# Two mixer stages folded into the feed-forward units block by block, with a unit's first side step ahead of the unit's own waits

## What is computed

```
h    = rms_norm(x) * (1 + scale1) + shift1
proj = h @ w_in                       # split over three causal mixers
out_a = rg_lru(conv(xa)) * gelu(ya)   # A, recurrent
out_b = forgetting_attention(rms_norm(fq), rms_norm(fk), fv, ff)   # B, "fox": 6 heads of 64
out_c = gated_linear_attention(gq, gk, gv, glow, gg)               # C, "gla": 4 heads, chunks of 64
x = x + gate1 * (concat(out_a, out_b, out_c) @ w_out)
h = rms_norm(x) * (1 + scale2) + shift2
x = x + gate2 * ((silu(h @ w_gate) * (h @ w_up)) @ w_down)
```

## Time and profile before

| | before |
|---|---|
| median of 3 runs | 3176.07 us (3166.4 to 3176.65) |
| profiled execution, its own time | 3180.37 us |
| span of the profile | 3178.6 us |
| share of the span: PE, DVE, ACT, POOL | 90%, 44%, 38%, 32% |
| mean granted TensorE clock | 0.925 of 2.4 GHz |

### The profile page before, as it was taken

How to read it: one execution, slowest core, us unless ns; L and a number is a source line. 1 busy time by engine, 2 the same in 40 slices (tenths; PEclk the granted TensorE clock), 3 DMA queues, 4 the chain that set the end, 5 groups by cost and what they waited for, 6 DMA issues and landing times.

```text
span 3178.6 us, 32439 instructions
## 1 busy us (share of the span) xinstructions
PE 2845.1 (90%) x12416; PEld 2258.7 (71%) x12416; DVE 1404.6 (44%) x1753; ACT 1206.8 (38%) x1601; POOL 1028.7 (32%) x466
## 2 busy tenths in 40 slices
PE   8899999935565579999999999998999999999999
PEld 4687878712344558888877887886878787778887
DVE  3878774543553543433334433334444443341112
ACT  3333242241523235354434445342444545232222
POOL 3545454400000023333333333333322223344443
PEclk9999999965556589999999999999999999999999
DMA  7555444357103424343444343443444343433233
GB/s 258 172 169 186 151 147 130 132 242 231 78 14 132 115 89 139 105 140 115 126 128 142 117 141 110 142 132 111 152 117 143 122 123 107 126 103 95 97 99 93
DMA packets 143866, 418.74 MB, mean 132 GB/s; under 512 B 16306, under 2 KB 18114, under 8 KB 137406
## 3 DMA queue, kind: packets, MB, share of 16 engines
q1 hardware_dynamic: 140848, 411.28, 40.7%
q10 hardware_dynamic: 2768, 5.24, 0.4%
q0 software_dynamic: 96, 0.15, 0.0%
HBM read 355.69 MB, written 60.92 MB: 131 GB/s over the span
## 4 chain that ended last, share of the span: by engine, by line
PE 59%; DVE 3%; issue 2%; DMA 2%; ACT 1%; SPq 1%; POOL 0%; DVEq 0%; ACTq 0%; POOLq 0%
PE ff_acc_ps L77 16%; PE ff_acc_ps L78 16%; PE ff_acc_ps L79 16%; PE fa_o_ps L1667 2%; PE fa_st_ps L1653 2%; PE fa_s_ps L1629 2%; PE fa_o_ps L1669 2%; PE fa_st_ps L1654 2%; PE fa_o_ps L1668 2%; PE fa_s_ps L1630 1%; DMA out_yT<-ff_gated 1%; DVE ff_silu L1480 1%; DVE ff_h_lo L1470 0%; DVE ff_rstd L1474 0%; DMA ff_silu<-mix_dram 0%
## 5 line engine op out<-in xcount | busy, mean ns | idle before, releaser
L1356 POOL TENSOR_TENSOR ff_w_lo<-ff_w_raw,ff_w_hi 128x1024 fp32r<-128x1024 f32 (+1 forms) x304 | 716.0, 2355 | 1450.1 <-PE ff_acc_ps L79 1422.5
L77 PE MATMUL ff_acc_ps<-ff_h_hi,ff_w_hi 128*128 128x512 f32 x1664 | 659.0, 396 | 42.8 <-DVE ff_h_lo L1470 21.4
L78 PE MATMUL ff_acc_ps<-ff_h_lo,ff_w_hi 128*128 128x512 f32 x1664 | 655.7, 394 | 0.0
L79 PE MATMUL ff_acc_ps<-ff_h_hi,ff_w_lo 128*128 128x512 f32 x1664 | 655.0, 394 | 0.0
L1365 ACT ACTIVATE ff_w_hi<-ff_w_raw 128x1024 fp32r<-128x1024 f32 (+1 forms) x304 | 315.6, 1038 | 853.2 <-PE ff_acc_ps L79 802.8
L77 PEld LDWEIGHTS ff_acc_ps<-ff_h_hi,ff_w_hi 128*128 128x128 f32 x1664 | 316.6, 190 | 117.4 <-issue 24.3
L79 PEld LDWEIGHTS ff_acc_ps<-ff_h_hi,ff_w_lo 128*128 128x128 f32 x1664 | 316.0, 190 | 68.2
L78 PEld LDWEIGHTS ff_acc_ps<-ff_h_lo,ff_w_hi 128*128 128x128 f32 x1664 | 316.7, 190 | 66.4
L1510 DVE TENSOR_TENSOR fa_p_lo<-fa_probs,fa_p_hi 128x512 fp32r<-128x512 f32 x240 | 146.5, 612 | 427.5 <-ACT fa_p_hi L1402 427.1
L209 POOL TENSOR_TENSOR w_lo<-w_raw,w_hi 128x1024 fp32r<-128x1024 f32 x96 | 240.0, 2502 | 272.5 <-PE g_ps L79 219.5
L77 PE MATMUL g_ps<-h_hi,w_hi 128*128 128x512 f32 x768 | 307.7, 401 | 16.9 <-POOL w_lo L209 12.8
(11 more groups left out here) (229 smaller groups left out, 3938.0 us busy)
## 6 DMA issues: line engine op xcount, KB each, us to landing
ff_w_raw<-in_w_gate_up SPq DMA_DIRECT2D x176, 512.0 KB, 3.8
w_raw<-in_w_in SPq DMA_DIRECT2D x96, 512.0 KB, 4.0
ff_w_raw<-in_w_down SPq DMA_DIRECT2D x64, 512.0 KB, 4.8
mod_w<-in_w_mod SPq DMA_DIRECT2D x24, 1024.0 KB, 5.5
fa_v<-v_split_dram SPq DMA_DIRECT2D x60, 384.0 KB
proj_dram<-stage SPq DMA_DIRECT2D x72, 256.0 KB, 3.2
ff_w_raw<-in_w_out SPq DMA_DIRECT2D x32, 512.0 KB, 4.9
fa_ks_a<-ka_dram SPq DMA_DIRECT2D x60, 256.0 KB
```

Source lines behind the costliest of these rows:

```text
L77: nc.tensor.matmul(out, hi, act_hi, start=first, stop=False)
L78: nc.tensor.matmul(out, hi, act_lo, start=False, stop=False)
L79: return nc.tensor.matmul(out, lo, act_hi, start=False, stop=last)
L1356: nc.gpsimd.tensor_tensor(w_lo[:, j % LO, wide], w_raw[:, j % RAW, wide], w_hi[:, j % HI, wide].bitcast(F32), ALU.subtract).then_inc(lo_re ...
```

## The change

`fox_operands` and `gated_linear_attention` are gone as functions of their own. The new `mix_and_feed_forward` does both for one block of 512 tokens at a time, as side steps: 7 steps "X" (operands) and 2 x 8 steps "G" (a head pair of mixer C). Block 0's 23 steps stand, one after another, ahead of the units and of block 0's attention. The steps of blocks 1, 2 and 3 stand one to a unit among the units of the block before (X in units 4 to 10, G in 14 to 29 for block 1, and 83 to 89 and 93 to 108 for block 2), and the block's attention turns follow in what is left: 34, 31 and 31 units. Carries (`f_carry`, `carry`) go from block to block. The buffers of X, of G, of attention and of the output projection's input share one region of SBUF, so each has to wait for the stores or the readers of the one before it (`operands_done`, `g_out`, `filled`, `heads_done`). The eight tiles of the output projection's input are now loaded together. The first turn of a unit now stands ahead of the unit's waits, and the others at even parts.

```diff
-def fox_operands(nc, vec, consts, fox_rows, proj, q_split, ka, kb, v_split):
...
-def gated_linear_attention(nc, vec, consts, w_alpha, proj, mix):
...
-def attend_and_feed_forward(nc, vec, mod, xT, w_out, w_gate_up, w_down, consts, mix, q_split, ka, kb, v_split, yT):
+def mix_and_feed_forward(nc, vec, mod, xT, w_alpha, w_out, w_gate_up, w_down, consts, fox_rows, proj, mix, q_split, ka, kb, v_split, yT):
...
+    X_STEPS, G_STEPS, X_LEAD, G_LEAD, A_LEAD, END = 7, 8, 3, 3, 2, 6
...
+    for b in range(NBLK):
+        turns = turns_of(b)
+        lo = -PRE if b == 0 else 1 if b == 1 else at["o", b - 1, KD - 1, 0] + 1
+        x_load.append(lo)
+        lo += X_LEAD
+        for s in range(X_STEPS):
+            side[lo + s] = [[("X", (b, s))]]
+        lo += X_STEPS + 1
+        g_load.append(lo)
+        lo += G_LEAD - 1
+        for j in range(GLA_T):
+            for s in range(G_STEPS):
+                side[lo + G_STEPS * j + s] = [[("G", (b, j, s))]]
+        lo += GLA_T * G_STEPS + 1
+        a_load.append(lo)
+        lo += A_LEAD - 1
+        hi = 0 if b == 0 else at["o", b, 0, 0] - END
         for x, turn in enumerate(turns):
             side.setdefault(lo + x * (hi - lo) // len(turns), []).append(turn)
...
+                def load_mix(b):
+                    heads_done(sp, b)
+                    for k in range(KD):
+                        sp.dma_start(mix_raw[:, k], mix[k, :, cols(b)]).then_inc(mix_in[k], 16)
...
+                    if kind == "G":
+                        b = n
+                        operands_done(sp, b)
+                        sp.dma_start(glow[:], proj[T_MISC, 0:GLA_RANK, cols(b)]).then_inc(glow_in, 16)
...
+                def ones(b):
+                    pool.wait_ge(g_out, 16 * GLA_T * (b + 1))
+                    nc.gpsimd.memset(q_b[HEAD_DIM:].bitcast(F32), 1.0).then_inc(filled, 1)
...
                     for x, turn in enumerate(turns):
-                        turn_at.setdefault((x + 1) * K // (len(turns) + 1), []).append(turn)
+                        turn_at.setdefault(x * K // len(turns), []).append(turn)
+                    for turn in turn_at.pop(0, []):
+                        attend(turn)
                     pe.wait_ge(lo_ready, j + 1)
```

More of the change, by code:

```diff
@@ new lines, in mix_and_feed_forward @@
+        with region:
+            qk, v_raw, sqr = there("fp_qk", [P, TILES, BLK]), there("fp_v_raw", [P, FOX_T, BLK]), there("fp_squares", [P, 3, BLK])
+            rows = [there("fp_rows%d" % i, [FF_ROW + FOX_HEADS, BLK]) for i in range(4)]
+            bias_hi, bias_lo = (there("fp_bias_" + n, [FF_ROW + FOX_HEADS, BLK], F32R)[FF_ROW:] for n in ("hi", "lo"))
+            qk_hi, qk_lo = there("fp_hi", [P, 2, BLK], F32R), there("fp_lo", [P, 2, BLK], F32R)
+            v_nat = there("fp_v_nat", [P, 2, 2, TPB, 3 * HEAD_DIM], F32R)
@@ new lines, in mix_and_feed_forward @@
+        region = ExitStack()
+        with region:
+            gk, gq, gv, gg = (there("ga_" + n, [P, GLA_T, BLK]) for n in ("gk", "gq", "gv", "gg"))
+            glow, restart = there("ga_glow", [GLA_RANK, BLK]), there("ga_restart", [P, BLK])
+            z, e_neg, one_e, b_cum, grow = (there("ga_" + n, [P, BLK]) for n in ("z", "e_neg", "one_e", "b_cum", "grow"))
+            v_n, k_n = there("ga_v_n", [P, TPB, P]), there("ga_k_n", [P, TPB, P])
+            att, state = there("ga_att", [P, 2, TPB, P]), there("ga_state", [P, NCH + 1, P])
@@ new lines, in mix_and_feed_forward @@
+        region = ExitStack()
+        with region:
+            mix_raw = there("ff_mix_raw", [P, KD, BLK])
+            raw_consts = there("fa_raw_consts", [P, 2, P])
+        mean, rstd12, newton = (r[0:HEADS2] for r in rows[:3])
+        logit, f_exp, log1p, f_err = (r[FF_ROW:FF_ROW + FOX_HEADS] for r in rows)
+        ones_row = ones_col[FF_ROW:FF_ROW + FOX_HEADS].to_broadcast([FOX_HEADS, BLK])
+        v_hi, v_ones, v_lo = (v_nat[:, :, :, :, i * HEAD_DIM:(i + 1) * HEAD_DIM] for i in range(3))
@@ L1320, in _ @@
                     if j == 0:
-                        for k in range(LRU_T, LRU_T + FOX_T):
-                            load_mix(0, k)
+                        load_mix(0)
                     kind, b, i, p = units[j]
@@ new lines, in prepare @@
+                def prepare(j):
+                    for b in range(NBLK):
+                        if j >= 0 and j in (x_load[b], g_load[b], a_load[b]):
+                            pool.wait_ge(lo_ready, j + 1)
+                        if j == x_load[b]:
+                            value_ones(b)
+                        if j == g_load[b]:
+                            zeros(b)
+                        if j == a_load[b]:
+                            ones(b)
+                for j in range(-PRE, 0):
+                    prepare(j)
```

1028 lines of the change are left out of this document (478 added, 550 removed).

## The result

The changed kernel takes 3192.9 us (median of 5 runs, 3187.0 to 3196.6) against 3173.2 for the kernel before (median of 5, 3166.4 to 3176.7). The ratio is 1.0063, 95% interval 1.0045 to 1.0081: slower by 0.6%, where 2.5% faster was forecast. The time lies outside the range.

A forecast was written before the change was run, and what follows sets the result against it. Units were taken as PE-bound, the serial stages as bound by chains of dependent steps. Terms -222 + 87 + 47 - 8 + 15 = -81 us gave a forecast of 3096 us, range 3035 to 3160.

The forecast's parts named there:

- Serial part: Block 0's operands, mixer C and attention ahead of the first unit: 260 us where 481.8 stood, -222 us.
- PE work in units: Operand and mixer C work of blocks 1 to 3 moved among the units: 29 us a block, +87 us.
- New waits: Waits that the moved steps put in front of the units: 15 to 16 us a block, +47 us.
- (a): X steps in units: PE waits for a row chain on ACT and DVE longer than a slot, 3 us a block.
- (e): M turns in units wait for DVE, which serves the unit before: 25 us in place of 15.3, 3 a block.
- Rival 2: Dense attention turns, up to 3.7 a unit, wait for Exp: +58, 3154 us; chance 0.17 shared with a falling clock.
- (b): G steps in units: sixteen state updates run late, about 1 us of wait at step 6; 2 us a block.
- (d): Start of a block's attention: store, memsets and first loads outlast two units, and weights come late; 6 us a block.
- Rival 5: Better than thought: the first step ahead of the unit's waits hides waits, block 0's chain takes 240: 3029 us, chance 0.10.
- The clock: Granted PE clock in the units falls by 0.007 from 0.99 through some 50 more waits: +15 us.
- Mix staging: Eight tiles of the output projection's input loaded together cost some 5 us where PE waited 13.1: -8 us.
- rival 1: Steps hold up the units in each of 75 slots: 3246 us at 2 us a slot, slower, chance 0.11.

The follow-up runs named there:

- e3: The changed kernel with SP's attention loads within a unit in the order in which their buffers come free: 3156.5 us, ratio 0.9961.
- e8: e4 with three query buffers in place of two: 3062.7 us, ratio 0.9653 to the kernel before.
- e10: The changed kernel with three query buffers in place of two and nothing else: 3144.3 us, ratio 0.9914.
- e1: The changed kernel with the old placement of turns, the first behind the unit's waits: 3165.5 us, ratio 0.9989.
- e4: The changed kernel with the edits of both e1 and e3: 3123.8 us, ratio 0.9858.
- e12: e8 with the changed kernel's placement of turns, the first ahead of the unit's waits: 3100.6 us, ratio 0.9763.
- e2: The kernel before with only the new placement of turns, the first ahead of the unit's waits: 3214.2 us, ratio 1.0154.
- e13: The kernel before with three query buffers and attention loads in the order in which buffers come free: 3136.3 us, ratio 0.9881.
- e14: e8 with attention ending ten units ahead of the next output projection in place of six: 3094.6 us, ratio 0.9754.
- e11: e8 with attention ending four units ahead of the next output projection in place of six: 3094.0 us, ratio 0.9749.
- e15: e8 with one unit more between mixer C's last step and attention's first turn in each block: 3090.6 us, ratio 0.9734.

## Why the prediction failed, point by point

**Serial part: right, in sum.** Forecast 260 us, measured 257.7. By its parts: the operands' last load gives way to mixer C's first product at 700.9 us, 61 us where 53 + 5 were forecast; mixer C and the start of attention end at the first score at 788.0, 87 us where 80 + 14 were; from there to the first unit 109 where 99 + 9 were. The parts miss by 3, -7 and 1, and so the 2 us of the whole is in part luck. In the last part attention took 95 us, and the first unit then waited 14.3 for `ff_h_lo`, where the 9 were to cover both its wait and its start. "ScalarE: Activation LUTs", "What ACT_TABLE_LOAD costs", in the Trainium skill puts 1.38 us on top of each switch. The serial part has 13 table loads and not 16, so by that rule it would have been some 18 us longer, an estimate; its rows show 1.28 us each, and the sum without a drain stood.

**PE work in units: 15 us short.** Of the 154.9 us of busy time that the stage gained, 47 are the clock and 6.2 the first passes, which before stood ahead of 1120.8; some 102 are left, forecast 87. The G steps came out as forecast: units 14 to 29, 93 to 108 and 169 to 184 take 21.3 to 21.9 us above their own 87.3, forecast 21.

**New waits: the step that failed.** The prediction's list (a) to (e) has no term for the loads of queries, keys and values during attention. Waits at lines 1500 and 1526 for these are 30.2 + 28.5 us where the kernel before has 11.0: 47.7 of the 79.9 us of idle time gained. Rival 2 looked at dense turns, and its sign named waits on `fa_kt`, but it was argued and priced by Exp on ACT, for which PE waits 1.7 us in all. e3, e8 and e10 show that the loads are what dense turns outrun, and the places of the waits for values agree: none in block 1, at 4.7 us a turn, 6.0 us in block 2 at 3.8, 22.5 in block 3 at 3.4. Of the terms that were listed, (e) M turns was right in what it measured, 23.5 for 25, (b) too, 6.3 for 6, and (d) 10.4 for 18 in the PE's waits. (a) was too small: 10.7 + 9.9 us for squares and rows in two blocks and 7.1 at the mean beside block 1's first steps (3.2 before), where 9 was forecast. The prediction took a step to have a unit; but with the PE's step first in its unit, and ACT's and DVE's last in theirs behind the norm of the tail units, it has half of that, and e1 gives the 2.7 us back at the spreads.

**"The first step ahead of the unit's waits" was priced only at M turns.** As a part of its own it costs 27, 33 and 38 us in the changed kernel (e1, e4 against e3, e8 against e12), and 45 in the kernel before (e2). Rival 5 counted it as a gain.

**The clock: a third of its size.** Forecast 0.99 to 0.983, +15; measured 0.97, +47. The prediction counted some 50 new waits and gave 0.3 us of clock for each; there are 75 waits of 0.3 us or more where there were 32, so 43 new ones, at 1.1 us of clock each. With 79.9 us of waits more, 0.6 us is lost for each microsecond waited. "TensorE: Matmul & The Clock Gate", Part 1, in the Trainium skill says that the lower level is the default and that activity releases it. This trace agrees in kind, with 0.50 right behind a wait and 1.00 later, and a wait nearly paid twice is nearer than my 15.

**Mix staging: larger than forecast.** The waits for `ff_h_lo` of line 1470 went in blocks 1 to 3 (block 0's is the 14.3 us above), and the 14 units around the output projection take 70.7 us at full clock where they took 79.2, 79.6 and 81.9: -29 in all, forecast -8. In the 29 are also 9.2 us of other waits that stood there, put down to issue and to `ff_w_lo`, and their clock.

**The sum.** Serial -224.1, units +234.8, start +0.6: the profiled execution is 11.3 us longer. (The medians differ by 19.7, since the profiled execution of the kernel before was 7 us above its median.) The gain was not lost in the 75 slots of rival 1, whose G steps cost what was forecast, but in the attention behind them (units 111 to 141 and 187 to 217: 331.5 and 389.4 us, in e8 301.1 and 343.3) and at the X steps.

**Is moving the steps worth it?** Yes, once attention doesn't wait for loads and turns stand behind the unit's waits: 3062.7 against 3136.3 for the kernel before with the same remedies (e8, e13), 74 us. That this is near the forecast of 81 is not a proof of its terms, several of which missed in both directions. The three causes on the changed kernel give 27, 36 and 49 us alone and 130 together. Of the queries' share most is no fault of the change, since the kernel before gains 35 us by them too. Against the 38.5 that it gains from both edits of SP's loads (e13), the 130 leave some 92 us, of the 101 between forecast and result, that the change itself brought.

**What stays open.** Why the same work in 27 units in place of 31 costs 32 us without late queries (e14). The waits name M turns, and block 1 loses as much as block 3, so I take the place of M turns inside a unit as the likely cause and not density. e11 and e15 point the same way: with two units more for attention and with one less, M turns wait 19.8 and 18.0 us, in e8 12.5. It stays not shown, as no run moved these turns alone. e8 may so owe part of its time to a favourable placement.

## What to carry to other kernels

When work that ran at its own pace is pressed into fewer slots, price the loads that come with each step: time from the last use of a buffer to its next first use, at the new pace, against issue plus landing, and look at what stands ahead of the load in its queue. A step that is first on one engine and last on the others has half a slot less than the plan says. And count the clock with the waits: here each new microsecond of PE waiting cost about 1.6.

## What was unexpected of the hardware

A wait of 2.62 us, over at 2438.0, cost about as much clock as one of 7.29 us, over at 2455.6. The windows show why: behind the short wait the clock fell only as PE began again, and behind the long one it fell in the middle of the wait, so that 4.0 of its 10.2 us at 1.2 GHz passed while PE stood and cost nothing.

```profile
2438.00:2444.80 6.80, 6.80 (x16) 5.24 (x17) 1.99 (x3) 1.08 (x2) 0.00 (x0) 0.50 0.00 0
2448.30:2451.60 3.30, 0.00 (x0) 0.00 (x0) 3.27 (x2) 0.00 (x0) 0.00 (x0) 1.00 0.59 145
2451.60:2461.80 10.20, 6.22 (x15) 4.76 (x16) 1.65 (x4) 2.14 (x3) 1.01 (x1) 0.50 0.41 121
```

PE was busy for 6.8 and 6.2 us of these two stretches at the lower level. What a wait costs in clock followed in these two cases from where the stretch fell, and not from the length of the wait.
